# A two-block transformer kernel on one core: the modulation's copies before the sine tables, the reciprocal moved, columns one step later

## The reference, cut to what matters

```python
mod = silu(c) @ ada_w[l] + ada_b[l]          # 6 * 1024 numbers: shift, scale, gate for mixer and experts
h   = rms_norm(x, norm_mix[l]) * (1 + scale) + shift
x   = x + gate * mixer(h)                    # layer 0: delta rule and sparse attention with rotary tables
```

## Time and profile before

| | us |
|---|---|
| median of 3 runs | 2700.13 (2698.55 to 2701.67) |
| the profiled execution's own time | 2702.49 |
| its span in the trace | 2700.8 |
| PE busy | 2494.3 (92%) |
| VectorE busy | 670.6 (25%) |
| ScalarE busy | 448.7 (17%) |
| mean granted clock of PE | 0.967 |

### The profile page before, as it was taken

The page is one execution under the profiler, slowest core; times in us unless marked ns, Lnnn a source line. Parts: engine busy times, 40 slices in busy tenths (PEclk is TensorE's granted clock), DMA queues, the critical chain, the costliest instruction groups (busy, mean ns, idle before and its releaser), DMA issues.

```text
span 2700.8 us, 28569 instructions
## 1 busy us (share of the span) xinstructions
PE 2494.3 (92%) x11612; PEld 1452.8 (54%) x11612; DVE 670.6 (25%) x1398; ACT 448.7 (17%) x812; POOL 0.2 (0%) x4
## 2 busy tenths in 40 slices
PE   6997899889988999989989899999999999999998
PEld 5855663333433685333333578785444777874443
DVE  2255241000112223101101244214211632133112
ACT  2322011000001211000000124102111233112111
POOL 0000000000000000000000000000000000000000
PEclk8998899999999989999999999999999999999999
DMA  9465638999999424899999742234999332247994
GB/s 392 148 255 191 232 118 352 428 430 428 429 429 417 146 73 179 362 429 428 429 428 428 336 156 94 94 143 185 420 424 424 150 133 104 76 187 284 427 422 188
DMA packets 53935, 769.55 MB, mean 285 GB/s; under 512 B 5984, under 2 KB 6496, under 8 KB 7008
## 3 DMA queue, kind: packets, MB, share of 16 engines
q1 hardware_dynamic: 53568, 768.17, 69.3%
q10 hardware_dynamic: 288, 0.26, 0.1%
HBM read 767.36 MB, written 1.05 MB: 285 GB/s over the span
## 4 chain that ended last, share of the span: by engine, by line
PE 75%; DMA 16%; DVE 6%; ACT 2%; issue 2%; SPq 0%; ACTq 0%; DVEq 0%
DMA slab<-in_experts 15%; PE psum L401 13%; PE psum L433 13%; PE psum L1883 12%; PE psum L1890 8%; PE psum L1913 7%; PE psum L1869 6%; PE psum L687 4%; PE psum L502 1%; PE psum L1201 1%; PE psum L509 1%; PE psum L1919 1%; PE psum L617 1%; PE psum L1903 0%; PE psum L1820 0%
## 5 line engine op out<-in xcount | busy, mean ns | idle before, releaser
L1883 PE MATMUL psum<-slab 128*64 128x512 f32 x2048 | 478.6, 623 | 76.9 <-DMA slab<-in_experts 44.3
L401 PE MATMUL psum<-slab 128*128 128x256 f32 (+6 forms) x1560 | 388.6, 407 | 10.8 <-ACT slab L2388 7.1
L1883 PEld LDWEIGHTS psum<-slab 128*64 128x64 f32 x2048 | 160.3, 143 | 374.6 <-issue 371.5
L433 PE MATMUL psum<-slab 128*128 128x256 f32 x1504 | 340.7, 390 | 13.3 <-DVE slab L2678 6.6
L1913 PE MATMUL psum<-slab 128*64 128x512 f32 x1536 | 345.4, 599 | 2.6 <-ACT slab L1949 2.6
L401 PEld LDWEIGHTS psum<-slab 128*128 128x128 f32 (+2 forms) x1560 | 274.1, 189 | 120.0 <-issue 71.8
L433 PEld LDWEIGHTS psum<-slab 128*128 128x128 f32 x1504 | 294.0, 196 | 58.6 <-issue 9.4
L1869 PE MATMUL psum<-slab 128*128 128x256 f32 x1024 | 249.3, 386 | 4.6 <-issue 2.4
L1890 PE MATMUL psum<-slab 128*64 128x512 f32 x1024 | 226.8, 595 | 3.1 <-DVE slab L1934 3.1
L1869 PEld LDWEIGHTS psum<-slab 128*128 128x128 f32 x1024 | 183.9, 190 | 73.9 <-issue 51.3
L1913 PEld LDWEIGHTS psum<-slab 128*64 128x64 f32 x1536 | 105.1, 137 | 207.5 <-issue 203.9
(11 more groups left out here) (429 smaller groups left out, 1612.2 us busy)
## 6 DMA issues: line engine op xcount, KB each, us to landing
slab<-in_experts SPq DMA_DIRECT2D x288, 2048.0 KB, 15.3
slab<-in_dense SPq DMA_DIRECT2D x73, 2048.0 KB, 8.6
slab<-in_dense SPq DMA_DIRECT2D x2, 1680.0 KB, 16.8
slab<-in_vec SPq DMA_DIRECT2D x1, 2635.5 KB, 39.9
slab<-in_dense SPq DMA_DIRECT2D x1, 1328.0 KB, 24.8
slab<-in_dense SPq DMA_DIRECT2D x2, 640.0 KB, 9.8
slab<-in_xT SPq DMA_DIRECT2D x1, 1024.0 KB, 8.1
out<-slab SPq DMA_DIRECT2D x2, 512.0 KB, 2.6
```

Of the source, the lines that this page charges most:

```text
L401: ins = mm(out_ap, lhs, rhs, start=(n == 0), stop=(n == len(pairs) - 1), skip_group_check=True)
L433: ins = mm(psum[:, b, S * j:S * j + S], narrow(s, width)[:, k, c0 + P * j:c0 + P * j + P], src[:, k, :], start=(k == 0), stop=(k == KD - 1 ...
L1883: ins = mm(psum[CAP * e:CAP * e + CAP, n, :], xg[:, k, CAP * e:CAP * e + CAP], sl(w[e], KD)[:, k, :], start=(k == 0), stop=(k == KD - 1), ...
```

## The change

Three things are done. On ScalarE the table activations move from before the four first steps to after the eight shifts of layer 0, and a wait for their own completion is put behind them. In each step ScalarE's copy of the rows stands before its copy of the last step's columns, and PE's rows stand before the columns of the last step, whose wait for the copy (`ada_copied`) comes later with them; `pe_ada_need` now stands ahead of both. The reciprocal leaves `dve_norm` for a function of its own, called right after VectorE's table arithmetic.

```diff
-        def dve_norm(q, gain, dst, done):
-
+        def dve_inverse_root(q):
             q.e.wait_ge(sems["root_ready"], q.due("root_ready"))
             q.skip("moment_ready")
             V.reciprocal(rstd[:, 0, :], rstd[:, 0, :]).then_inc(sems["dve_step"], 1)
             q.e.wait_ge(sems["dve_step"], q.due("dve_step"))
+
+        def dve_norm(q, gain, dst, done):
+
             for k in range(KD):
...
         def pe_ada(q, steps, b):
 
             for _ in range(steps):
+                pe_ada_need(q, q.ada - 1)
+                pe_ada_rows(q, b + q.ada % 2)
                 if q.ada_bank is not None:
                     pe_ada_columns(q, q.ada - 1, q.ada_bank)
-                pe_ada_need(q, q.ada - 1)
                 q.ada_bank = b + q.ada % 2
-                pe_ada_rows(q, q.ada_bank)
                 q.ada += 1
...
         def act_ada(q, steps, b):
             for _ in range(steps):
+                act_ada_rows(q, q.ada, b + q.ada % 2)
                 if q.ada_bank is not None:
                     act_ada_columns(q, q.ada - 1, q.ada_bank)
                 q.ada_bank = b + q.ada % 2
-                act_ada_rows(q, q.ada, q.ada_bank)
                 q.ada += 1
...
             ins.then_inc(sems["table_ready"], 1)
+            q.e.wait_ge(sems["table_ready"], q.due("table_ready"))
...
             act_root(q, rstd[:, 0, :], psum[:, 7, 0:S])
-            act_tables(q)
             act_ada(q, ADA_FIRST, 0)
             act_ada_end(q)
             for l in range(2):
                 act_shift(q, hT, modc[:, 0:8])
                 if l == 0:
+                    act_tables(q)
                     act_even(q)
...
             dve_tables(q)
+            dve_inverse_root(q)
             q.skip("unit_done", ADA_FIRST)
```

## The result

The changed kernel takes 2691.88 us (median of 11 runs, 2688.02 to 2697.66) against 2701.90 (11 runs, 2698.55 to 2710.12): ratio of the times 0.9959, 95% interval 0.9947 to 0.9972, a gain of 11 us with 7.6 to 14.3 in the interval. The forecast of 2691.9 was a gain of 8.2 us from 2700.13, the median of the first three runs of the kernel before. The profiled execution took 2693.34 with a span of 2691.7: 9.1 us under the profiled one of before.

A forecast was written before the change was run, and what follows sets the result against it. PE was taken to have three quarters of the chain, transfers most of the rest. Terms 5.3 + 1.8 + 0.4 + 0 + 0.7 = 8.2 us, off the median 2700.13, gave 2691.9; range 2687.8 to 2697.0.

The forecast's parts named there:

- three signs of being wrong: Rows start off the landings; clock from 28 to 45 differs; first experts' matmuls move by less than 7.5 us.
- low-clock rival: Opening: PE at low level behind slot waits, rows 3 and last columns slow; costs 3.3, gain 4.9 us, 2695.2; chance 0.18.
- Part 1: Opening: last read 5.3 us earlier with loads ending last, moved reciprocal 1.8 us; first feature matmul at 34.1.
- Part 2: PE's clock in the opening: taken as zero, bounds -3.3 and +2.5 us.
- Part 3: Three steps beside the rope: dots then wait for VectorE's rope; gain 0.4 us, bounds -0.8 to +0.4.
- Part 4: Five steps beside the search for keys: PE 2.7 us less, but VectorE comes last; gain 0.
- Part 5: Twelve single steps in inverse and scan: 0 from the reordering, 0.7 us gained at one place.
- The gain after the fifth step: Inverse: PE's wait for the copy after the fifth step is filled with columns 3; 0.7 us.
- The seams: Single steps in inverse and scan: exposed loads or pipeline starts, 0.1 us each, in all 1.1 either way.
- swallowed: Whole run: transfers follow their own pace, an earlier even stage only waits longer for experts; 2700.1; chance 0.06.
- The slower case: Scan: new order lets the clock sit low, six rows and six columns cost 14.8 us; 2706.7; chance 0.04.
- The full clock: Gap before the features too short for a fall, first unit takes 6.9; gain 10.7 us, 2689.4; chance 0.20.

The follow-up runs named there:

- tables alone: Kernel before with only the table activations, and the wait for their completion, moved behind the shifts; ratio 0.9982, 4.9 us.
- no waits for slots: Changed kernel with the first four steps all reading slot 0, PE waiting for slots 1 to 3 only after the last columns; ratio 0.9963.
- the order alone: Kernel before with only rows put ahead of columns in every step, tables still ahead of the first copy; ratio 0.9980, 5.4 us.
- opening-alone: Changed kernel with the old order of rows and columns in all steps behind the first four; ratio 0.9971, 7.8 us.
- filled pair: Kernel before and changed kernel, each with unused PE products in gaps of the opening; first feature matmul at 38.63 and 34.60.
- The filler before the dots: Changed kernel with unused PE products in the opening, plus two of 128x512 between the third step beside the rope and the dots; ratio 0.9962.
- filled before: Kernel before with unused PE products behind the first rows (five) and the last columns (three and a half); ratio 0.9978, 5.9 us.
- filled: Changed kernel with unused PE products in three gaps of the opening; ratio 0.9952, median 2690.56 us.
- the reciprocal alone: Kernel before with only the reciprocal moved up behind VectorE's table arithmetic; ratio 1.000 (0.9989 to 1.001).

## Why the prediction came out right, step by step

The time came out right, the mechanism only in part. That 2691.9 stands beside 2691.88 is luck: the forecast took 8.2 us off 2700.13, and eleven runs each put the gain at 11 us, from 2701.90. All three signs of being wrong that the prediction names have come: rows 3 started at 29.40 and not at their landing of 28.4, the clock was 0.50 from 30 to 32, and the first experts moved by 5.06 us and not by 7.5. Up to the first experts, the first two traces set side by side show the gain of the prediction's low-clock rival (4.9 us), not that of the forecast.

- **Part 1, the starts.** Landings, the move of the copy, of the reciprocal and of the tables were as forecast: rows 2 at 23.58 to 23.70 in the five traces of the changed opening, rows 3 at 28.49 and features at 34.20 in the trace in which the clock was back for them. That loads end last was tried from both sides (tables alone; no waits for slots). That the tables alone, or the order alone, bring nearly all of it I had not said. One reading was not in its row: the prediction has the activation start at once behind the table load, but there it stood 2.70 us waiting for VectorE's arguments. The changed kernel's timeline does show it: the load is at 39.49 for 1.28 us, the first sine at 40.78, so the 2.66 us per switch that the prediction quotes do not show here.
- **Part 2, the clock.** This is the term that was mis-sized. I took zero for what the clock takes and gives, with the falls of one trace as the norm. The rival of the low clock behind the slots happened: features at 36.82 and 37.80, 2.7 and 3.7 us later than 34.1 (its price was 3.3). But I had read the kernel before at its better end: 41.21, and 45.58 in its repeat. The means of two and two are 43.4 and 37.3, 6.1 us; with the opening-alone trace as a third of the new kind, 36.3 and 7.1 us, which was the forecast's number by another road. At the first experts, behind the whole first mixer, the two traces of before stand at 389.79 and 394.19 and the two of the changed kernel at 384.73 and 384.84: 7.2 us in the mean. Few traces, so this is a size and not a proof; that the clock has its own share is shown by the filled pair (4.0 us, clock 1.00 in both) and by the 5.9 us of fillers in the kernel before.
- **Part 3, the rope.** Rope's start to dots was 11.04 in all six traces with the old order and 10.70 to 10.72 in all six with the new one: 0.33 us against 0.4. The releaser is VectorE, as said. The timeline of the changed kernel's second trace, which answers to the earlier trace rows:

```profile
173.25 2.19 PE L959 MATMUL psum<-slab 64*128 64x256 f32 x14 [2.19 <-DVE slab L948]
```

  The idle time was 2.19, not 1.4, since the three steps were done sooner than I summed. Rope's start to relu, 12.22 to 12.45 in the old order, was 11.88 or 12.83 in the new: in three of the five unfilled waits the dots ran low, the case behind the lower bound of that term (-0.8; 0.6 us lost in the relu's start). The filler before the dots gave 11.88.
- **Part 4** is confirmed: nothing came from the five steps; VectorE still came last (its copy of the result, L1117, at 203.74 with no wait ahead of it).
- **Part 5, the single steps.** From the first product of the inverse (L1201) to the last columns, the old order took 94.77 to 95.40 us in five traces (97.38 in the filled before), the new one 93.18 to 93.25 in four and 95.19, 95.50 in two. The gain after the fifth step is 28.75 - 28.28 = 0.47 of the 0.7 forecast. The seams are inside their 1.1: the product ahead of the fifth step begins 22.25 instead of 22.02 us behind the first one, and the stretch from the last wide product (L1245) to the last columns takes 42.3 to 42.4 us in all six traces with the new order in place of 41.8 in all six with the old. The rest, up to 2.2 us, is the stretch from the fifth step to that last wide product: 24.82 us in both traces of before, 22.59 and 22.53 in both of the changed kernel. The timeline of PE, first before, then after:

```profile
269.58 5.46 PE L1201 MATMUL psum<-slab 128*128 128x128 f32 x32 [0.26 <-ACT slab L518]
286.72 4.17 PE L1240 MATMUL psum<-slab 128*128 128x256 f32 x16
```

```profile
266.37 3.84 PE L1204 MATMUL psum<-slab 128*128 128x128 f32 x32 [0.26 <-ACT slab L520]
281.52 3.93 PE L1243 MATMUL psum<-slab 128*128 128x256 f32 x16
```

  The 32 products behind the fifth step (L1201) ran low before and high after. PE had waited 0.72 us for a copy ahead of them, and now has columns there. They took 5.46 or 5.47 us in all six traces with the old order and 3.84 in four of six with the new; in the other two (no slot waits, filled) they ran low again. So the order makes the fall rarer in these traces and does not remove it; six traces do not settle by how much.
- **The sum.** 6 to 7 us of the opening, 0.3 at the dots less what a low clock takes, and 0 to 2 us in the inverse and scan give 6 to 9.5. Timed were 11.1 and, in the repeat, 9.4. The forecast's 8.2 lies in the intervals of both. What remains goes with the clock. In the 71 runs of the kernel before that were timed beside the experiments, a run is 1.9 us shorter for each 0.001 that its mean granted clock is higher, with 1.4 us of scatter about that line. By that line the repeat of the changed kernel (nine runs, in the mean 9.7 us under the runs of before beside it) is 5.8 us faster at the same clock, and 3.9 us go with its mean clock of 0.9687 against 0.9666. The same line leaves 2.0 us to the reciprocal alone and 1.1 of 6.0 us to the fillers in the kernel before. This is an estimate, good to about 1.5 us: by so much the kernel before, timed once more as an experiment of its own, lies off the line. By it the forecast's 8.2 has two errors that pull apart: the waits are worth less (about 6 us in the changed kernel as it runs), and the clock, put at nothing, gives some 4 us over the whole run. In which stretches the clock is higher, and why, stays open; stretches far behind the change move by 3 us between two traces of the kernel before.
- **The rivals.** The shift was not swallowed: the 5.0 us at the first unit's copy are 5.06 at the first experts. The slower case did not come: from the first product of the inverse on, one step's rows ran low in every trace (2.56 to 3.59 us), in either order, and no more. The full clock from 16 to 50 us came only with fillers.

## What to carry to other kernels

When a wait goes, read from the landings of the next transfers what ends last then: here the loads of slots 2 to 4 capped a gain that the engines' own steps would have made larger, and two edits that bring 5 us each bring little more than 5 together. A trace of one execution holds one draw of PE's clock at every gap; before a term is summed from it, ask which of its durations are at 0.50, and price both kernels at both levels. Products that nobody reads, in gaps of known length, separate the clock's share from that of the waits; so does setting each run's time against its mean granted clock, with the unchanged kernel as a measure of the error.

## What the runs showed of the hardware

- Two executions of the same kernel differ by 4.4 us in the first 46 us, and PE's granted clock is what differs: rows at the low level three times in one, once in the other.
- PE's clock fell ahead of 24 us in the tables-alone kernel with no gap above 0.86 us since 15.5; it held through three gaps of 0.72 us from 30 to 38 in the first trace of before, and stayed low through the same gaps in the second.
- The clock also falls where PE has no gap. In the changed kernel it was 1.00 before 96 us, 0.50 from 98 to 100 and back by 102 with PE busy throughout, behind 32 matmuls of 12 columns (L401, 3.7 us). It cost 1.7 us (29.41 for 27.73 in the chain for the same 128 matmuls). The order alone (30.03) and the kernel before with fillers (29.41) had the same fall; the other nine traces kept 27.73, with the same matmuls ahead. The Trainium skill, "TensorE: Matmul & The Clock Gate", section "What's actually happening", has the clock follow how busy the engine has been lately; this trace agrees in the gaps of the opening, and here, where the profile shows PE busy throughout, it does not say what was missing.
- The same transfer in the same queue (slot 4) landed at 33.2 to 33.5 us in seven of the twelve traces and at 34.3 to 34.6 in five, while slot 3 landed at 28.3 to 28.6 in eleven and at 29.6 in one.
